# A hybrid decoder step: the first stage's weight splits, small tile and TensorE order rearranged

## The reference, cut to what matters

```python
def layer_norm(x, g, b):
    mu = mean(x, -1); var = mean((x - mu)**2, -1)
    return (x - mu) * rsqrt(var + 1e-5) * g + b

xp = layer_norm(concat([meta_tokens, x_prompt]), ln0_g, ln0_b)   # 16 + 512 tokens, 1024 features
xs = layer_norm(x_sample, ln0_g, ln0_b)                          # 8 tokens
h  = x @ w_in                    # 1024 -> 4768 columns: latents, retention q/k/v/gate, branch gates
...                              # latent attention, retention, merge, LN1
a, g = split(x @ w_ffn_in)       # then a causal depthwise convolution of width 3 with conv_w, conv_b
y = LN2(alpha*x + (gelu(conv(a)) * g) @ w_ffn_out)
```

## Time and profile before

| | us |
|---|---|
| median of 3 runs | 1014.45 |
| lowest and highest | 1013.73, 1018.99 |
| span of the profiled execution | 1027.7 |
| TensorE busy in that span | 974.2 (95%) |
| VectorE busy | 666.5 (65%) |
| ScalarE busy | 387.2 (38%) |
| GpSimd busy | 39.1 (4%) |

### The profile page before, as it was taken

How to read it: one execution, slowest core, us unless ns; L and a number is a source line. 1 busy time by engine, 2 the same in 40 slices (tenths; PEclk the granted TensorE clock), 3 DMA queues, 4 the chain that set the end, 5 groups by cost and what they waited for, 6 DMA issues and landing times.

```text
span 1027.7 us, 22122 instructions
## 1 busy us (share of the span) xinstructions
PE 974.2 (95%) x9086; PEld 898.9 (87%) x9086; DVE 666.5 (65%) x1054; ACT 387.2 (38%) x857; POOL 39.1 (4%) x44
## 2 busy tenths in 40 slices
PE   4899999999999999599999999999999999999995
PEld 3899999988888897455569999999999999999995
DVE  7467556765555555888837658697774335767567
ACT  4234332324151514333323323556661124565331
POOL 0000000000000011333100000000000000000000
PEclk9899999999999999899999999999999999999998
DMA  9504444313233324999643934224323243341643
GB/s 256 169 24 106 122 122 108 89 23 102 50 96 85 105 102 158 383 344 354 243 161 118 281 85 125 82 82 115 90 82 93 81 114 83 94 111 56 190 119 124
DMA packets 174772, 136.88 MB, mean 133 GB/s; under 512 B 18707, under 2 KB 162936, under 8 KB 170328
## 3 DMA queue, kind: packets, MB, share of 16 engines
q1 hardware_dynamic: 166442, 93.47, 32.5%
q0 software_dynamic: 5760, 37.75, 9.8%
q10 hardware_dynamic: 2502, 4.68, 1.2%
HBM read 124.18 MB, written 11.80 MB: 132 GB/s over the span
## 4 chain that ended last, share of the span: by engine, by line
PE 78%; DVE 12%; issue 4%; ACT 3%; DMA 1%; ACTq 0%; DVEq 0%; another core or an unknown queue 0%; POOL 0%; POOLq 0%
PE PS L2014 34%; PE PS L2242 8%; PE PS L2694 8%; PE PS L2756 6%; PE PS L2025 3%; PE PS L2471 3%; DVE w_lo L1225 2%; PE PS L2589 2%; PE PS L2414 2%; ACT p_sample L972 2%; PE PS L2279 1%; PE PS L2268 1%; PE PS L2340 1%; DVE y_tok L1734 1%; PE PS L2256 1%
## 5 line engine op out<-in xcount | busy, mean ns | idle before, releaser
L2014 PE MATMUL PS<-x_hi,w_hi 128*128 128x262 f32 (+1 forms) x744 | 164.0, 292 | 2.7 <-DVE x_lo L1272 1.4
L1225 DVE TENSOR_TENSOR w_lo<-w_raw,w_hi 128x2048 fp32r<-128x2048 f32 (+3 forms) x65 | 125.9, 1937 | 59.7 <-ACT w_hi L703 48.2
L2014 PE MATMUL PS<-x_lo,w_hi 128*128 128x262 f32 (+1 forms) x744 | 160.0, 287 | 0.0
L2014 PE MATMUL PS<-x_hi,w_lo 128*128 128x262 f32 (+1 forms) x744 | 159.6, 286 | 0.0
L703 ACT ACTIVATE w_hi<-w_raw 128x2048 fp32r<-128x2048 f32 (+3 forms) x59 | 94.5, 1601 | 145.9 <-PE PS L2014 88.3
L2014 PEld LDWEIGHTS PS<-x_hi,w_hi 128*128 128x128 f32 x744 | 120.7, 190 | 6.0 <-issue 2.4
L2014 PEld LDWEIGHTS PS<-x_lo,w_hi 128*128 128x128 f32 x744 | 120.1, 190 | 0.0
L2014 PEld LDWEIGHTS PS<-x_hi,w_lo 128*128 128x128 f32 x744 | 120.0, 190 | 0.0
L2242 PE MATMUL PS<-x_hi,w_hi 128*128 128x262 f32 (+1 forms) x256 | 78.7, 307 | 0.0
L2242 PE MATMUL PS<-x_hi,w_lo 128*128 128x262 f32 (+1 forms) x256 | 73.3, 286 | 0.0
L2242 PE MATMUL PS<-x_lo,w_hi 128*128 128x262 f32 (+1 forms) x256 | 73.3, 286 | 0.0
(11 more groups left out here) (376 smaller groups left out, 2293.2 us busy)
## 6 DMA issues: line engine op xcount, KB each, us to landing
w_raw<-in_w_ffn_in_dram SPq DMA_DIRECT2D x44, 512.0 KB, 4.5
w_raw<-in_w_in_dram SPq DMA_DIRECT2D x37, 512.0 KB, 6.7
w_raw<-in_w_ffn_out_dram SPq DMA_DIRECT2D x28, 320.0 KB, 3.8
w_raw<-in_w_o_dram SPq DMA_DIRECT2D x12, 512.0 KB, 5.2
w_raw<-in_w_ffn_out_dram SPq DMA_DIRECT2D x16, 384.0 KB, 3.9
gate_scratch<-gate_out ACTq DMA_DIRECT2D x8, 524.0 KB, 2.9
gates<-gate_scratch SPq DMA_DIRECT2D x8, 524.0 KB, 9.0
x_T_scratch<-x_sum_T SPq DMA_DIRECT2D x1, 2144.0 KB, 7.5
```

Of the source, the lines that this page charges most:

```text
L1225: V.tensor_tensor(WL[:, at_, ks], RAW[:, at_, ks], WH[:, at_, ks].bitcast(F32), ALU.subtract).then_inc(s_wsplit, 1)
L2014: last = T.matmul(PS[:, bank, 0:n], w[:, par, kw + k, m * P:(m + 1) * P], x[:, k0 + k, half * n:(half + 1) * n], start=start and k == 0 an ...
```

## The change

Ahead of the first stage's products:

- ACT's queue loads only the identity (64 KB, own semaphore `unit_landed`) and the five groups of norm vectors; the other four square constants go to SP's queue behind `conv_rows` (one more count of `consts2_landed`); the four DMAs of `conv_w` and `conv_b` go to Pool's queue (`conv_w_landed`).
- Pool normalises tile 0 (`x0_scaled` in, `x0_normed` out) and then makes the low parts of weight slots 0 and 1. VectorE drops both `lo` and the normalisation of tile 0, and takes over the rounding of slot 0 to its high part (`WH[:, 0]`) from ScalarE.
- VectorE's eight small `feat` instructions of tile 0 become two over all features (`feat_first`), the second of them SBUF on SBUF.
- TensorE turns tiles in the order 1, 0, 2; it turns the convolution vectors behind them; both column tiles of slot 0 for half 0 are done before `x_forward(3)` and `x_forward(4)`. 26 products of the identity with itself, into an unused part of PSUM, are put ahead of and between these steps (`keep_warm`: 8, 4, 8 and 6).
- Two lists of semaphores are made shorter, with no other effect, and the count on which the first store of y waits is one lower.

The core of the diff:

```diff
+            sp.dma_start(SQ[:, 1:5, :], consts["square"].ap()[:, 1:5, :]).then_inc(c2, 16)
...
-            y_out = Count(S["x_normed"], start=2 * NT)
+            y_out = Count(S["x_normed"], start=2 * NT - 1)
...
+            for j in range(3):
+                pool.dma_start(VR[j * FT:(j + 1) * FT, 1, :],
+                               ins["conv_w"][0, j].rearrange("(k p) -> k p", p=P)).then_inc(S["conv_w_landed"], 16)
+            pool.dma_start(VR[3 * FT:4 * FT, 1, :],
+                           ins["conv_b"][0].rearrange("(k p) -> k p", p=P)).then_inc(S["conv_w_landed"], 16)
+            pool.wait_ge(S["x0_scaled"], 1)
+            nc.gpsimd.tensor_scalar(XK[0:T0, 0, :], XK[0:T0, 0, :], MV[0:T0, 0, 0:1], RSV[0:T0, 0:1], ALU.subtract, ALU.mult
+                                    ).then_inc(S["x0_normed"], 1)
+            for n in range(2):
+                pool.wait_ge(s_whi, n + 1)
+                nc.gpsimd.tensor_tensor(WL[:, n], RAW[:, n], WH[:, n].bitcast(F32), ALU.subtract).then_inc(s_wsplit, 1)
...
-            act.dma_start(SQ[:], consts["square"].ap()).then_inc(S["consts_landed"], 16)
+            act.dma_start(IDENT, consts["square"].ap()[:, 0, :]).then_inc(S["unit_landed"], 16)
...
-            for j in range(3):
-                act.dma_start(VR[j * FT:(j + 1) * FT, 1, :],
-                              ins["conv_w"][0, j].rearrange("(k p) -> k p", p=P)).then_inc(S["consts_landed"], 16)
-            act.dma_start(VR[3 * FT:4 * FT, 1, :],
-                          ins["conv_b"][0].rearrange("(k p) -> k p", p=P)).then_inc(S["consts_landed"], 16)
...
-            hi(0, first=True)
+            landed[0].add(2)
...
+            def feat_first():
+                x0 = XS[:, :, 0:T0]
+                dve.wait_ge(S["ln_turned"], 2)
+                V.tensor_tensor(x0, PS[:, 2, 0:KT * T0].rearrange("p (k c) -> p k c", k=KT),
+                                LN0[:, 0:KT].unsqueeze(2).to_broadcast([P, KT, T0]), ALU.mult).then_inc(chain.sem, 1)
+                dve.wait_ge(chain.sem, chain.after())
+                V.tensor_tensor(x0, x0, LN0[:, KT:2 * KT].unsqueeze(2).to_broadcast([P, KT, T0]), ALU.add
+                                ).then_inc(S["x_feat_dve"], 1)
             x_stats(0)
             x_stats(1)
-            x_norm(0)
+            dve.wait_ge(std.sem, std.after())
+            V.reciprocal(RSV[0:T0, 0:1], SDV[0:T0, 0:1]).then_inc(S["x0_scaled"], 1)
             x_norm(1)
             x_stats(2)
             dve.wait_ge(fd[0].sem, fd[0].after())
             V.tensor_copy(LN0[:], PS[:, 0, 9:9 + 2 * KT]).then_inc(S["ln0_ready"], 1)
+            V.tensor_copy(VT[:], PS[:, 0, 0:9]).then_inc(S["vectors_T_ready"], 1)
             x_norm(2)
-            V.tensor_copy(CV[:], PS[:, 1, 0:4 * FT])
-            V.tensor_copy(VT[:], PS[:, 0, 0:9]).then_inc(S["vectors_T_ready"], 1)
+            dve.wait_ge(s_win[0], 32)
+            V.tensor_copy(WH[:, 0], RAW[:, 0]).then_inc(s_whi, 1)
             dve.wait_ge(S["ln0_ready"], 1)
-            feat(range(KT), 0, 0)
+            feat_first()
             feat(range(4, KT), 1, 2)
-            lo(0)
             feat_lo(0, COL_A)
             feat_lo(4, COL_A)
             x_stats(3)
             x_stats(4)
             x_norm(3)
             x_norm(4)
+            dve.wait_ge(S["conv_w_turned"], 1)
+            V.tensor_copy(CV[:], PS[:, 1, 0:4 * FT]).then_inc(S["vectors_T_ready"], 1)
             feat(range(4, KT), 3, 4)
             feat_lo(0, COL_B)
             feat_lo(4, COL_B)
             vt = Count(S["vectors_T_ready"])
-            dve.wait_ge(vt.sem, vt.after())
+            dve.wait_ge(vt.sem, vt.after(2))
             dve.wait_ge(S["conv_turned"], 1)
             V.tensor_copy(PV[:].rearrange("p f c -> p (f c)"), PS[:, 3, 0:2 * DEC * FT]).then_inc(S["conv_taken"], 1)
-            lo(1)
+            whi.add(2)
...
-                pe.wait_ge(normed.sem, normed.after())
+                if t:
+                    pe.wait_ge(normed.sem, normed.after())
+                else:
+                    pe.wait_ge(S["x0_normed"], 1)
...
-            pe.wait_ge(c1.sem, c1.after(10))
-            T.transpose(PS[:, 0, 0:9 + 2 * KT], VR[0:9 + 2 * KT, 0, :], IDENT[0:9 + 2 * KT, 0:9 + 2 * KT])
-            T.transpose(PS[:, 1, 0:4 * FT], VR[0:4 * FT, 1, :], IDENT[0:4 * FT, 0:4 * FT]).then_inc(s_fd[0], 1)
-            for t in range(3):
+            def keep_warm(n):
+                for _ in range(n):
+                    T.matmul(PS[:, 3, 3 * P:4 * P], IDENT, IDENT, start=True, stop=True, skip_group_check=True)
+            pe.wait_ge(S["unit_landed"], 16)
+            keep_warm(8)
+            pe.wait_ge(c1.sem, c1.after(5))
+            T.transpose(PS[:, 0, 0:9 + 2 * KT], VR[0:9 + 2 * KT, 0, :], IDENT[0:9 + 2 * KT, 0:9 + 2 * KT]).then_inc(s_fd[0], 1)
+            keep_warm(4)
+            for t in (1, 0, 2):
                 x_forward(t)
+            pe.wait_ge(S["conv_w_landed"], 16 * 4)
+            T.transpose(PS[:, 1, 0:4 * FT], VR[0:4 * FT, 1, :], IDENT[0:4 * FT, 0:4 * FT]).then_inc(S["conv_w_turned"], 1)
+            keep_warm(8)
...
+                tile(0, 1, 8, XH, XL, 0, 1, halves=(0,))
                 x_forward(3)
-                tile(0, 1, 8, XH, XL, 0, 1, halves=(0,), ks=range(4))
                 x_forward(4)
-                tile(0, 1, 8, XH, XL, 0, 1, halves=(0,), ks=range(4, 8))
-                pe.wait_ge(c2.sem, c2.after(8))
+                keep_warm(6)
+                pe.wait_ge(c2.sem, c2.after(9))
                 rows = CN[:].rearrange("p a b -> p (a b)")
                 for f in range(FT):
                     last = T.transpose(PS[:, 3, 16 * f:16 * f + 16], rows[:, f * P:(f + 1) * P], IDENT[0:16, 0:16])
                 last.then_inc(S["conv_turned"], 1)
+                pe.wait_ge(S["vectors_T_ready"], 2)
                 pe.wait_ge(x_split.sem, x_split.after())
                 tile(0, 0, 8, XH, XL, 0, 0, halves=(1,), ks=range(4))
                 pe.wait_ge(x_split.sem, x_split.after())
```

15 lines of the change are left out of this document (7 added, 8 removed).

## The result

The changed kernel takes 1026.76 us (median of 17 runs, 1023.58 to 1028.54). The kernel before, run beside it, takes 1018.99 us (17 runs, 1013.73 to 1025.80). The ratio is 1.0076, with a 95% interval of 1.0062 to 1.0091: slower by 0.76%, where 1010.7 was forecast, and above the range's upper end of 1016.2.

A forecast was written before the change was run, and what follows sets the result against it. TensorE was taken as the bound, with at most 18 us to win in the first 45 us. The reordering's -3.2 and the clock's -0.6 us summed to -3.8, giving 1010.65 (forecast 1010.7), range 1007.0 to 1016.2.

The forecast's parts named there:

- Bounds: Whole kernel: TensorE bounds it behind the first 45 us, so gains there, at most 18 us, reach the end unchanged.
- the 3.8 us of gain: First stage: 3.2 us from the new TensorE order plus 0.6 us from the clock, giving 1010.65 us.
- The reordering: TensorE, first stage: column tile 1 of half 0 ahead of x_forward(3) ends x_forward(4) at 28.1, not 31.28; gain 3.2 us.
- nothing gained: First stage: VectorE's gain given back and TensorE late at x_forward(3), or a late landing; 0 to -1 us; chance 0.10.
- Pool's prices: Pool, first stage: 1.8 times VectorE's time, so 4.1 us for a split and 1.4 for tile 0.
- Exclusion: Pool and VectorE, first stage: at full-width SBUF access each waits for the other's whole instruction; VectorE's gain is given back.
- a wake-up takes time: First stage: Pool wakes too slowly to get ahead of feat_first's second instruction, which asks after only 0.35 us.
- The slower rival: First stage: Pool gets in first, its split holding feat_first's second instruction; half 1 at 36.2, total 1015.65; chance 0.20.
- VectorE's own terms: VectorE, first stage: tile 2 normalised at 12.9, rounding 1.63 us, feat_first 0.35 each, feat ending at 17.15 against 17.73.
- TensorE in the first stage: x_forward(3) starts at 26.3, x_forward(4) ends at 28.1, and half 1 starts 4.3 us later at 32.45.
- Clock: Half 1's first products: unit products shorten the idle gap before them; -1.8 to +0.6 us, middle -0.6 taken.

The follow-up runs named there:

- e9: Changed kernel with tile 0's normalisation and both splits back on VectorE, slot 0's rounding on ScalarE, tiles in order 0, 1, 2: 1022.02 us, ratio 1.0030.
- y3b: Kernel before plus 105 TensorE instructions (26 small products, one semaphore increment) where TensorE waits anyway: 1025.22 us, ratio 1.0074.
- y1: Changed kernel plus 151 TensorE instructions hidden in a wait, making the total shift against the kernel before 256: 1019.57 us, ratio 1.0010.
- e8_before: Kernel before, unchanged, timed against itself in a session of the lower level: 1019.27 us, ratio 1.0018, span 1016.4.
- e10: Kernel before with only TensorE's order changed, both column tiles of half 0 ahead of the turns of tiles 3 and 4: 1017.77 us, ratio 0.9990.
- e5_after: Changed kernel, unchanged, beside the kernel before in a session of the upper level: 1029.57 us, ratio 1.0009.
- x4_after: Changed kernel, unchanged, beside the kernel before in another session of the upper level: 1030.29 us, ratio 1.0022.
- e1: Changed kernel without the 26 unit products, against the kernel before at the upper level: 1030.94 us, ratio 1.0052.
- y2: Changed kernel without unit products and without elementwise work on Pool, against the kernel before at the lower level: 1016.55 us, ratio 0.9986.
- e6_before: Kernel before, unchanged, timed against itself for a trace at the upper level: 1029.32 us, ratio 1.0013.

## Why the prediction was wrong

**Bounds: the step that failed.** The prediction said that what is won in the first 45 us "arrives at the end as a rigid shift, since TensorE is then the bound". It took the edit's reach to be the stage it rewrites. The shift of start times is indeed rigid: `e9` begins its gathered stage 3.5 us before the changed kernel, for the 3.5 us of half 1. But the edit also moved every later TensorE instruction by 105 places in its list, and the stage at 408 to 518 us, whose instructions this moved, is 7.4 us longer (5.1 of them in the gaps). This is a term that the sum put at nothing without a reason. `y3b` shows it alone (1.0074 with only the 105 hidden instructions added), `y1` takes it away (1.0010).

**The base.** The forecast lies 16.1 us below the measured 1026.76, and 4.5 of these are the base: 1014.45 was the median of 3 runs, where 17 gave 1018.99. The other parts are the 3.8 us of gain that did not come and the 7.8 of loss. The sum was also made against a profile of the upper level and carried over to a median of the lower one. The stage in question differs between them: 111.5 us in the first trace of before, 102.5 in `e8_before`. The gaps of after weigh most where before has none. And half 1 at 35.64 was the latest of before's four traces, 33.24 to 35.64. Against `e8_before` the forecast 32.45 would have been a gain of 0.8 us, not 3.2.

**The reordering,** put at 3.2 us, is worth nothing measurable: `e10` 0.9990 (0.9968 to 1.0012), half 1 at 33.71 against 33.24. The 1.80 and 2.34 of the earlier trace rows for `x_forward(3)` and its 12 products were those of a low clock (0.66 from 25 to 30 us in that trace). In `e8_before`, the same kernel, they take 1.07 and 1.49. And TensorE reached `x_forward(3)` late in the new order, at 27.59 in `e10`, since column tile 0 took 5.96 us and column tile 1 another 3.21 ahead of it. The prediction had allowed 0.9 us for the rest of column tile 0 behind the second x_lo. But already in the earlier trace rows this tile ends at 24.27, 1.9 us behind x_lo (22.40), and in the changed kernel its 24 products run at a granted clock of 0.50 for 5.72 us and end at 25.22, 2.7 us behind x_lo (22.53). That TensorE would come late is what the prediction gave to "nothing gained", though it looked for the cause in column tile 1.

**Pool's prices.** The split was put at 4.1 us and took 4.50 and 4.59, near the 4497 ns cited with the prediction. By the prediction's own chain, in which both splits stand one behind the other, 0.4 us more for each makes 0.8 us and not the 0.4 that it gave. Tile 0 was put at 1.4 us by the ratio of the earlier trace rows and took 3.78. The ratio came from a write of one column and does not carry over to 1024 elements on 24 partitions.

**Exclusion.** It was assumed, and holds beside Pool's two splits, as does the lock cited with it: 4.50 us for a 192-element instruction inside the first and 2.77 for a normalisation of 0.81 inside the second. It is not general: the statistics run inside the second split at full speed, and beside the scaling of tile 0 (3.78 us) tile 1's normalisation lost 0.49 us and was not held to Pool's end. What I had wrong is who gets in first. The forecast let `feat_first` ask before Pool ("a wake-up takes time"); Pool woke 0.22 us earlier. The slower rival had the held second instruction of `feat_first` as its mark, and it is met: the record begins at 13.69 but ends with Pool's split. Its size was off: 36.2 was given for half 1, and it came at 34.72. The rival had a chance of 0.20 and was right in the first stage; its total, 1015.65, lacked the gathered stage like every other case.

**VectorE's own terms.** The rounding of slot 0 took 1.22 us (1.63 forecast), `feat_first`'s first half 0.35 (0.35), tile 2 was normalised at 12.25 (12.9). They were right or better, and were lost in the 4.15 us that the lock cost next.

**TensorE in the first stage.** The chain shows that behind the held instruction the 48 products of half 0 set the start of `x_forward(3)`, at 28.24; tile 3 is normalised at the same moment, 28.19. `x_forward(4)` ended at 30.27 (28.1 forecast) and half 1 came 2.3 us late: the distance of 4.3 us between them was right, at 4.45.

**Clock.** -0.6 us was put in; in the trace of the result it was 0. The first 24 products of half 1 take 4.75 us as in the earlier trace rows (4.77), and 36 to 39 us is at granted clock 0.52 in the changed kernel (start:end, length, PE, PEld, DVE, ACT, POOL, granted clock):

```profile
19.50:25.02 5.52, 5.52 (x24) 5.52 (x25) 5.49 (x9) 3.24 (x3) 1.97 (x1) 0.50 1.03 163
36.00:39.00 3.00, 3.00 (x16) 3.00 (x15) 0.42 (x2) 0.00 (x0) 0.00 (x0) 0.52 0.92 274
```

In spite of the unit products both stretches that they were meant to warm run at 1.2 GHz here. That is not so in every execution: in `e5_after`, the same kernel, the 24 products take 3.21 us at a granted clock of 1.00, 1.5 us less, and 4.74 again in `x4_after`. Without unit products they take 4.77 or 4.78 in all four traces of before, 5.43 in `e1` and 3.25 in `y3b`. So the size of this term changes from one execution to the next, and what part the unit products have in it no run isolates. No run shows a gain in the total from them: `y2` without any is at 0.9986, `e9` with all of them at 1.0030.

**Where the 0.76% lies.** Before the gathered stage +1.1 us, in it +7.4, behind it 0.0: +8.5 of span in two profiles, beside 7.8 in the medians. The 1.1 is within what traces of one kernel differ by: the first piece is 407.1 to 409.5 us in four traces of before and 404.8 to 408.2 in three of the changed kernel. `e9`, without Pool's arithmetic, has 404.7.

**What stays open.** Why there are two levels. The chip does not decide it: sessions 3 and 6 have the same chip number in the record, and before took 1018.11 in the one and 1026.36 in the other. What differs can be seen, once an element, where a product spreads the maximum (L2445) and ScalarE takes it. In `e6_before` (upper level):

```profile
454.88 1.42 PE PS L2445 x2
456.32 0.18 ACT sm L968
```

and in `e8_before` (lower level):

```profile
462.59 0.33 PE PS L2445 x2
462.94 0.19 ACT sm L968
```

In all traces of before at the upper level ScalarE starts 1.0 to 1.1 us after the product's end, in five elements each; in every trace of the lower level it is 0.04 us. Added up, that is about 5.5 of the 9 us between the levels. What holds ScalarE up no row names. It also offers a reason why the two kernels are equal at the upper level: in `x4_after` the elements in which TensorE has a gap (453.5 and 466.6 us) have only the 0.04 us, as if one wait hid the other. This is read off traces and was not tried. The 1.0052 of `e1` at the upper level is not explained. And the record shows packets and gaps, not the fetcher itself: that TensorE was short of instructions is inferred from the packets' timing, from the distance of 512 between the gaps, and from `y1` and `y3b`.

## What to carry to other kernels

An unrolled stage of very short instructions can be limited by instruction fetch at one position and not at another, so an edit that adds or removes instructions on an engine can cost or win time hundreds of microseconds later; compare the lengths of all stages, not only of the one that was edited, and when an untouched stage has changed, add hidden instructions until the shift is a multiple of 256 and measure again. Filler on the busiest engine is not free even where it fills a wait. Elementwise work moved to Pool can hold a VectorE instruction on SBUF operands until it ends (4.50 us for one of 0.35), so put it where VectorE has PSUM work or nothing to do, and look in the trace at which instructions it holds.

## What the runs showed of the hardware that I had not expected

- TensorE idled up to 1.5 us at the same products in element after element, with the granted clock at 1.00, and every gap of the table above ended 2.2 to 2.6 us after the start of a 16 KB packet on the instruction queue. The gaps of one trace lie 512 records apart.
- 105 instructions ahead of an unchanged stage of 102.5 us made it 110.8 us; 256 made it 105.9 in one kernel, with none of those gaps.
- A bare semaphore increment on TensorE cost about 0.16 us: 105 held its first product until 17.45, 256 until 40.76.
- A scaling of 24 partitions by 1024 elements took 3.78 us on Pool, whose first elementwise instruction it was, and 0.80 on VectorE in `e8_before`.
- The kernel before measured 1018 us in three of the seven sessions and 1026 to 1029 in four. The difference lies in the gathered stage: 102.5 us against 111.5 to 115.8 in three traces, and at the upper level ScalarE takes the spread maximum 1.0 to 1.1 us late in each element.
